# Softmax normalisation of both attentions moved from VectorE to ScalarE, with the inverse of the row sums made one head ahead

## The reference

```
first block:   scores = q k^T / 8 + bias by relative position   (keys limited to the chunks so far)
second block:  scores = q k^T / 8 + c_i - c_j                   (c: running sum of log_sigmoid of a gate, keys j <= i)
both:          p = softmax(scores over the keys);  o = p v
```

## Time and profile before

| | |
|---|---|
| median of 3 executions | 2767.97 us (2766.33 to 2770.85) |
| the profiled execution | 2766.05 us, span of its instructions 2764.1 us |
| mean granted TensorE clock | 0.938 of full |
| TensorE busy (matmul) | 2495.0 us, 90% |
| VectorE busy | 1801.5 us, 65% |
| ScalarE busy | 964.4 us, 35% |
| GpSimd busy | 1469.9 us, 53% |

### The profile page before, as it was taken

How to read it: one execution, slowest core, us unless ns; L and a number is a source line. 1 busy time by engine, 2 the same in 40 slices (tenths; PEclk the granted TensorE clock), 3 DMA queues, 4 the chain that set the end, 5 groups by cost and what they waited for, 6 DMA issues and landing times.

```text
span 2764.1 us, 36708 instructions
## 1 busy us (share of the span) xinstructions
PE 2495.0 (90%) x12718; PEld 1986.0 (72%) x12718; DVE 1801.5 (65%) x2200; ACT 964.4 (35%) x1494; POOL 1469.9 (53%) x1234
## 2 busy tenths in 40 slices
PE   4978989978999998999497789999996889999998
PEld 3754777856777776878386558888885778888887
DVE  6769866757787875667687857665137945666324
ACT  2013257742444432777312323222014631222102
POOL 4730334426555552344365126676779937666675
PEclk8977989989999998999798789999998999999999
DMA  8735569953333323899432113332241023333222
GB/s 312 261 131 205 190 241 331 325 176 92 99 99 93 98 83 116 282 337 311 141 81 80 65 54 92 105 93 89 98 125 47 32 67 94 91 103 95 95 88 84
DMA packets 319122, 386.73 MB, mean 140 GB/s; under 512 B 51578, under 2 KB 259214, under 8 KB 318902
## 3 DMA queue, kind: packets, MB, share of 16 engines
q1 hardware_dynamic: 261424, 335.84, 37.1%
q10 hardware_dynamic: 34438, 28.08, 3.3%
q0 software_dynamic: 23168, 21.59, 2.4%
HBM read 397.62 MB, written 55.41 MB: 164 GB/s over the span
## 4 chain that ended last, share of the span: by engine, by line
PE 35%; POOL 20%; issue 18%; DVE 14%; DMA 9%; ACT 2%; SPq 0%; ACTq 0%; POOLq 0%; DVEq 0%
POOL WL L837 14%; PE PAIR L529 6%; PE PAIR L530 5%; PE PAIR L531 5%; POOL WH L833 5%; PE PAIR L1842 4%; PE BANK L529 2%; PE BANK L530 2%; PE BANK L531 2%; DMA RAW<-in_ffn_w_up 2%; DMA RAW<-in_moe_w 2%; PE PAIR L1812 2%; DVE ADA_SUM L634 1%; PE BANK L2288 1%; DVE ADA_SUM L632 1%
## 5 line engine op out<-in xcount | busy, mean ns | idle before, releaser
L837 POOL TENSOR_TENSOR WL<-RAW,WH 128x512 fp32r<-128x512 f32 x584 | 815.1, 1426 | 12.2
L529 PE MATMUL PAIR<-HH,WH 128*128 128x512 f32 x1792 | 712.5, 398 | 56.1 <-POOL HL L1126 29.9
L530 PE MATMUL PAIR<-HL,WH 128*128 128x512 f32 x1792 | 702.6, 392 | 0.0
L531 PE MATMUL PAIR<-HH,WL 128*128 128x512 f32 x1792 | 702.1, 392 | 0.0
L832 POOL TENSOR_TENSOR TURN<-ONES 128x1 f32<-128x1 f32 x146 | 33.6, 230 | 890.0 <-PE PAIR L531 811.5
L529 PEld LDWEIGHTS PAIR<-HH,WH 128*128 128x128 f32 x1792 | 339.7, 190 | 140.9 <-issue 44.2
L530 PEld LDWEIGHTS PAIR<-HL,WH 128*128 128x128 f32 x1792 | 340.0, 190 | 71.4 <-issue 2.4
L531 PEld LDWEIGHTS PAIR<-HH,WL 128*128 128x128 f32 x1792 | 339.5, 189 | 71.8
L833 POOL TENSOR_SCALAR WH<-RAW 128x2048 fp32r<-128x2048 f32 x146 | 284.9, 1951 | 0.0
L2022 POOL DMA_INDIRECT XG<-htok_scratch,GATHER_I x78 | 107.1, 1373 | 257.3 <-PE PAIR L1812 151.3
L529 PE MATMUL BANK<-WH,GH 128*128 128x256 f32 x624 | 181.1, 290 | 0.0
(11 more groups left out here) (530 smaller groups left out, 4841.7 us busy)
## 6 DMA issues: line engine op xcount, KB each, us to landing
RAW<-in_moe_w SPq DMA_DIRECT2D x156, 512.0 KB, 7.0
RAW<-in_ffn_w_up SPq DMA_DIRECT2D x88, 512.0 KB
W2RAW<-in_moe_w SPq DMA_DIRECT2D x78, 512.0 KB, 6.1
ADA_B<-in_ada_w SPq DMA_DIRECT2D x30, 1024.0 KB, 5.3
RAW<-in_ssm_w_in SPq DMA_DIRECT2D x48, 512.0 KB
ADA_A<-in_ada_w SPq DMA_DIRECT2D x18, 1024.0 KB, 7.7
RAW<-in_ffn_w_down SPq DMA_DIRECT2D x32, 512.0 KB
RAW<-in_ev_w_in SPq DMA_DIRECT2D x20, 512.0 KB
```

The lines of the kernel that those rows point to most:

```text
L529: nc.tensor.matmul(o, wh, xh, start=start, stop=False)
L530: nc.tensor.matmul(o, wh, xl, start=False, stop=False)
L531: return nc.tensor.matmul(o, wl, xh, start=False, stop=stop)
L837: ins = pool.tensor_tensor(WL[:, s, c], RAW[:, s, c], WH[:, s, c].bitcast(F32), ALU.subtract)
```

## The change

`normalise` moves to ScalarE. It is four activations of the function Identity with the inverse sums as a scale per row, in place on S. VectorE keeps only `invert`, the reciprocal, with its own semaphore `inverse`. VectorE now does `invert(0)` ahead of the loop and `invert(h + 1)` at the start of head h's turn. ScalarE does `normalise(0)` ahead of its loop and `normalise(h + 1)` ahead of `copy(h)`. In the first attention TensorE's `turned(h)` at odd heads from 3 on gets a wait of its own for `dve_ada_end` of the head before, since the wait for `probs`, which used to come from VectorE, no longer implies it.

```
@@ -1300,7 +1300,7 @@
     SEG = [0, P, 3 * P, 6 * P]
     HOME = {3: (0, 0), 2: (1, 0), 0: (1, 3 * P), 1: (2, 0)}
     PT_HOME = {0: (0, 0), 1: (1, 0), 3: (1, 3 * P), 2: (2, 0)}
-    att_sems = [{s: sem(f"att{n}_{s}") for s in ("scaled", "exp", "probs", "turned", "out")} for n in range(2)]
+    att_sems = [{s: sem(f"att{n}_{s}") for s in ("scaled", "exp", "inverse", "probs", "turned", "out")} for n in range(2)]
 
 
 
@@ -1342,6 +1342,9 @@
 
         def turned(h):
             bank = take_bank(pe, att_bank(n, h, 3))
+            if n == 0 and h % 2 and h > 1:
+
+                pe.e.wait_ge(ada_added, h // 2)
             if n == 0 and h % 2 == 0 and h:
 
                 pe_ada(pe, 5 + h // 2, bank[:, 2 * P:])
@@ -1396,13 +1399,9 @@
             dve.link(ins)
             dve.e.tensor_scalar(MX[:, h % 2, 1, :], MX[:, h % 2, 0, :], -1.0, None, ALU.mult).then_inc(w["scaled"], 1)
 
-        def normalise(h):
+        def invert(h):
             dve.wait(w["exp"])
-            dve.link(dve.e.reciprocal(SUMS[:, h % 2, :], SUMS[:, h % 2, :]))
-            for j in range(NT):
-                seg = s[:, h % 2, SEG[j]:SEG[j] + P * (j + 1)]
-                ins = dve.e.tensor_scalar(seg, seg, SUMS[:, h % 2, j:j + 1], None, ALU.mult)
-            ins.then_inc(w["probs"], 1)
+            dve.e.reciprocal(SUMS[:, h % 2, :], SUMS[:, h % 2, :]).then_inc(w["inverse"], 1)
 
         def rest(i):
             dve.wait(hi_ready)
@@ -1419,8 +1418,10 @@
 
         scale(0)
         scale(1)
+        invert(0)
         for h in range(HEADS):
-            normalise(h)
+            if h + 1 < HEADS:
+                invert(h + 1)
             if n == 0:
                 ada_pieces(h)
             elif h:
@@ -1447,6 +1448,13 @@
                 seg = s[:, h % 2, SEG[j]:SEG[j] + P * (j + 1)]
                 ins = act.e.activation(seg, seg, ACT.Exp, bias=MX[:, h % 2, 1, j:j + 1], accum_out=SUMS[:, h % 2, j:j + 1])
             ins.then_inc(w["exp"], 1)
+
+        def normalise(h):
+            act.wait(w["inverse"])
+            for j in range(NT):
+                seg = s[:, h % 2, SEG[j]:SEG[j] + P * (j + 1)]
+                ins = act.e.activation(seg, seg, ACT.Identity, scale=SUMS[:, h % 2, j:j + 1])
+            ins.then_inc(w["probs"], 1)
 
         def high(i):
             act.wait(w["out"], 2)
@@ -1468,7 +1476,10 @@
 
         exponential(0)
         exponential(1)
+        normalise(0)
         for h in range(HEADS):
+            if h + 1 < HEADS:
+                normalise(h + 1)
             copy(h)
             if h + 2 < HEADS:
                 exponential(h + 2)
```

## The result

The kernel with the change takes 2780.91 us (median of five executions, 2779.16 to 2783.85), the kernel before 2767.97 (2766.33 to 2770.85). The ratio is 1.0047, with a 95% interval of 1.0032 to 1.0061. It is **12.9 us slower**, and the interval lies wholly above the 0.2% that can be told from no change.

The account below looks back on a forecast made before the run. VectorE was taken to bound the kernel in both attentions. The first attention's +8.4 us and the second's +6.6 made 15.0 on 2766.05, so 2781; the median lies 1.9 above that execution, forecast 2782 us, range 2774 to 2795.

Parts of the forecast that it names:

- The wait at the reciprocal: VectorE stands still for head h + 1's exponentials, 2.42 us, 2.70 with signal and reciprocal, seven times in each attention.
- The turns: VectorE's turns of heads 1 to 5 grow: +4.2 us in the first attention, +3.9 in the second.
- VectorE's waits for scores: Waits for TensorE's scores within turns go; with `dve_ada_end` 2.3 us in the first attention, 2.6 in the second.
- The starts: Head 0's transposes come later in each attention, behind head 1's exponentials: +2.9 us in the first, +2.8 in the second.
- The tails: After head 5's turn to the last `rest`: +1.3 us in the first attention, -0.1 in the second.
- The new wait of TensorE for `dve_ada_end`: At odd heads it ends 0.2 us into the turn, with TensorE still busy or shortly after: costs nothing.
- The busy times: VectorE's falls by some 20 us to about 1782, ScalarE's rises by some 35 to 1000.
- The sum: Both attentions together: 8.4 + 6.6 = 15.0 us on the profiled execution's 2766.05.
- The clock rival: TensorE's clock stays down at 1.2 GHz in the attentions: +20 us on top, 2802; chance 10%.
- The faster rival: Exponentials are done when VectorE arrives, so each turn is 1.2 us shorter: -11 us, 2755; chance 5%.

Follow-up runs that it names:

- the late reciprocals: The change with head h + 1's reciprocal moved behind turn h's ADA pieces or table work, and ScalarE's multiplication behind the copy: 2754.21 us.
- the late place: Behind turn h's ADA pieces or table work; the kernel before with VectorE's whole normalise(h + 1) moved there, one head ahead: 2762.13 us.
- nothing a head ahead: The change with VectorE inverting head h at the start of turn h and ScalarE multiplying head h ahead of copy(h): 2813.42 us.
- head 0's ahead: The late reciprocals plus head 0's reciprocal inside scale(1), its multiplication ahead of head 1's exponentials: 2746.31 us, again 2744.54 us.

## Why the prediction was right

- **The wait at the reciprocal.** I forecast 2.42 us and 2.70 with the reciprocal, fourteen times. There were fourteen waits, with 2.15 to 2.36 us of idle time. In a plain turn it was 2.35, or 2.44 from where VectorE's next instruction could have started (225.11) to where the reciprocal did. That this wait opens each turn is shown by the trace. That it costs time is shown by the late reciprocals, where one of the fourteen waits is left (2.28 us in head 0's turn of the second attention) and the kernel is faster than before.
- **The turns.** Forecast 11.40 and 10.87 in the first attention, 10.29 in the second. They were 11.26 (216.29 to 227.55), 10.79 and 10.11. A turn took in 2.44 us of wait and 0.09 of reciprocal, 2.53 and not 2.70. Of the 0.17, 0.11 are the reciprocal's price, 0.03 the signal's, and 0.03 a rounding: 2.42 + 0.05 + 0.2 is 2.67. VectorE's waits for scores are gone from the turns behind head 0's, as forecast.
- **The starts.** Forecast +2.9 and +2.8, measured +2.7 and +2.7, with ScalarE's multiplication at 1.92 against my 1.93. The Trainium skill's rule to keep multiplications on VectorE (ScalarE: Activation LUTs, Rules for kernel authors) is right about the single operation, 1.92 against 1.27 us. It does not decide here: in the late place the kernel is some 8 us faster with them on ScalarE than with them on VectorE.
- **The tails.** Forecast +1.3 and -0.1, measured +2.0 and +0.5. In the first the ADA pieces kept VectorE waiting 2.38 and 1.25 us. They came 9.8 and 13.7 us into the tail where I had 10.1 and 12.8. In the second `rest` waited 0.86 us for ScalarE's last half, so there TensorE's chain ended last. In two further profiles of the second attention in its new form that wait is not there, and the tail is 0.3 us shorter than before. The new wait of TensorE for `dve_ada_end` shows as no lost time in VectorE's turns with the change (TensorE stood idle for about 0.5 us ahead of 236.10 and 258.80).
- **The busy times.** VectorE's was forecast at about 1782 us and was 1778.5. ScalarE's was forecast to rise by some 35 and rose by 28.8, since I took 2.2 us a head there, without the overlap that I had used for the price of 1.93.
- **The sum.** 15.0 forecast, 14.8 between the two profiles, 12.9 between the medians. That 15.0 and 14.8 agree so closely is in part luck: the turns came out 0.5 and 0.8 us below the forecast, the tails 0.7 and 0.6 above it. So is part of the 1.1 us between 2782 and 2780.91. The base was 1.9 us below the median, so that 15.0 on the median is 2783 and not 2782. And it was one execution whose attentions were fast, as the other profiles show (80.3 and 77.9 us against 77.9 and 76.6). In the first attention the difference is mostly the wait for an ADA piece in head 0's turn, in the second waits for scores within turns, which I let vanish from the base as 2.6 us.
- **The clock rival** did not come. The granted clock in the windows stayed at 0.74 and 0.78. It came nearer where transposes were late as well, at 0.64 and 0.59 with nothing a head ahead. The Trainium skill (TensorE: Matmul & The Clock Gate, Why this matters for your kernels) names gaps between bursts of matmuls as what costs the clock. The group behind the longest gap was slow here too: 1.94 us for eight transposes behind 6.59 us of idle time at 204.64, against 1.07 at the full clock. But with the change TensorE was idle for 22.8 of 88 us in the first window, before for 13.0 of 80, and the mean clock was the same, so the gaps alone did not decide it. Why one head runs at 1.2 GHz and the next at 2.4 was not settled.
- **The faster rival** did not come with the order as printed, where each plain turn waited 2.35 us. The late reciprocals show that it was a question of place: freed work does count once VectorE need not wait for ScalarE's answer to its last instruction.

## What to carry to other kernels

When work moves from one engine to another and the first must hand over a small result, look at what the handing instruction waits for at its new place in the queue. If that is the other engine's answer to the instruction just ahead, the two engines run in turn, and the round trip (here 2.4 us) replaces the work saved (1.3). Put the handing instruction behind independent work that is as long as the answer, and order the other engine's queue so that work which nobody waits for stands last. The runs here moved both at once; the second half of the rule was not tested apart.

## What the runs showed that I had not expected

- At the lower clock TensorE is as much a bound of these attentions as VectorE: with nothing a head ahead VectorE waited 3.36 and 1.02 us of a 13.5 us turn for scores. How much of the gain of the earlier transposes is the clock's was not measured apart. The windows' mean granted clock in the first attention went from 0.64 (transposes behind exponentials and multiplications), through 0.74, to 0.82 with head 0's ahead and 0.86 in its second profile. The same form also varies: the change's first attention had 0.74, 0.73 and 0.78 in three profiles.
- A reciprocal of four columns takes 0.17 us, but VectorE starts an instruction that does not need its result 0.08 to 0.12 us after it began. With a wait for the result it is 0.2.
- The kernel before varies by 13 us in 20 executions of one set (2760.47 to 2773.99 us). Single profiles of its attentions differ by 2.4 us.
